# Feed-forward output tiles in pairs from seven block products of sums, in place of eight plain ones

## The reference, cut to what matters

```
x  = x + rmsnorm(mix @ w_o, g_post_mix)
hf = rmsnorm(x, g_pre_ff)
ff = square(relu(hf @ w_ff1 + b_ff1)) @ w_ff2 + b_ff2     # 1024 -> 4096 -> 1024, float32
x  = x + rmsnorm(ff, g_post_ff)
```

## Time and profile before

| | |
|---|---|
| timed runs (3) | 1230.9 us median, 1230.79 to 1233.1 |
| profiled execution | span 1229.2 us from first to last instruction; the page gives no whole time of its own for it |
| PE busy | 1222.8 us (99%), 9103 matmuls |
| DVE busy | 732.4 us (60%), 1031 instructions |
| ACT busy | 508.6 us (41%), 783 instructions |
| POOL busy | 65.2 us (5%), 129 instructions |
| chain that ended last | PE 99% |
| granted TensorE clock | 1.000 |

### The profile page before, as it was taken

The page is one execution under the profiler, slowest core; times in us unless marked ns, Lnnn a source line. Parts: engine busy times, 40 slices in busy tenths (PEclk is TensorE's granted clock), DMA queues, the critical chain, the costliest instruction groups (busy, mean ns, idle before and its releaser), DMA issues.

```text
span 1229.2 us, 23577 instructions
## 1 busy us (share of the span) xinstructions
PE 1222.8 (99%) x9103; PEld 1153.2 (94%) x9103; DVE 732.4 (60%) x1031; ACT 508.6 (41%) x783; POOL 65.2 (5%) x129
## 2 busy tenths in 40 slices
PE   9999999999999999999999999999999999999998
PEld 9999978989797897989999999999999999999998
DVE  6933788888888888887455434338543112443334
ACT  7533433353454335335443212246654223454222
POOL 4020001101100110110000000000000000000000
PEclk9999999999999999999999999999999999999999
DMA  6353225516432551623222222322322222222222
GB/s 221 103 168 138 70 81 214 195 34 239 166 118 89 215 184 34 239 104 103 93 96 87 86 86 85 144 101 62 95 100 88 85 100 70 88 91 95 86 68 73
DMA packets 40341, 141.23 MB, mean 115 GB/s; under 512 B 4788, under 2 KB 7220, under 8 KB 40168
## 3 DMA queue, kind: packets, MB, share of 16 engines
q1 hardware_dynamic: 28456, 99.02, 23.6%
q0 software_dynamic: 11424, 41.23, 9.6%
q10 hardware_dynamic: 416, 0.35, 0.1%
HBM read 118.31 MB, written 22.26 MB: 114 GB/s over the span
## 4 chain that ended last, share of the span: by engine, by line
PE 99%; issue 0%; DVE 0%; ACT 0%; POOL 0%; POOLq 0%
PE product L1655 89%; PE side L1655 10%; PE side L1840 0%; PE side L1830 0%; ACT y L1012 0%; DVE asmp L1205 0%; DVE u L1135 0%; POOL ones L446 0%; POOL eps L445 0%; DVE u L1132 0%; POOLq L2122 0%
## 5 line engine op out<-in xcount | busy, mean ns | idle before, releaser
L1029 DVE TENSOR_TENSOR wlo<-wraw,whi 128x1024 fp32r<-128x1024 f32 x176 | 214.9, 1224 | 205.8 <-ACT whi L578 191.2
L1655 PE MATMUL product<-ahi,whi 128*128 128x256 f32 (+1 forms) x1392 | 294.0, 290 | 1.3 <-DVE asmp L1205 1.3
L1655 PE MATMUL product<-ahi,wlo 128*128 128x256 f32 (+1 forms) x1392 | 290.2, 288 | 0.0
L1655 PE MATMUL product<-alo,whi 128*128 128x256 f32 (+1 forms) x1392 | 287.9, 286 | 0.0
L578 ACT ACTIVATE whi<-wraw 128x1024 fp32r<-128x1024 f32 x176 | 184.3, 1052 | 245.7 <-PE product L1655 170.5
L1655 PEld LDWEIGHTS product<-ahi,whi 128*128 128x128 f32 x1392 | 223.7, 188 | 11.6 <-issue 10.6
L1655 PEld LDWEIGHTS product<-alo,whi 128*128 128x128 f32 x1392 | 224.0, 188 | 0.0
L1655 PEld LDWEIGHTS product<-ahi,wlo 128*128 128x128 f32 x1392 | 222.8, 188 | 0.0
L1242 DVE SCALAR_TENSOR_TENSOR accp<-u,wdw,accp 128x512 f32<-128x512 f32 x240 | 163.7, 745 | 0.7 <-DVE accp L1242 0.7
L1655 PE MATMUL product<-hidhi,whi 128*128 128x288 f32 (+1 forms) x512 | 111.2, 289 | 0.0
L1655 PE MATMUL product<-hidlo,whi 128*128 128x288 f32 (+1 forms) x512 | 111.0, 288 | 0.0
(11 more groups left out here) (319 smaller groups left out, 1739.4 us busy)
## 6 DMA issues: line engine op xcount, KB each, us to landing
wraw<-in_wstream SPq DMA_DIRECT2D x176, 512.0 KB, 3.5
crg<-in_c_in POOLq DMA_DIRECT2D x32, 512.0 KB, 6.6
out_c_s<-crg POOLq DMA_DIRECT2D x32, 512.0 KB, 3.1
hb<-head_rows POOLq DMA_DIRECT2D x4, 580.0 KB, 5.3
x<-in_xT SPq DMA_DIRECT2D x4, 544.0 KB, 6.4
sgm<-in_xT SPq DMA_DIRECT2D x1, 2176.0 KB, 8.0
out_c_p<-cst POOLq DMA_DIRECT2D x4, 512.0 KB, 8.1
out_yT<-y SPq DMA_DIRECT2D x4, 288.0 KB, 2.2
```

The lines of the kernel that those rows point to most:

```text
L1029: V.tensor_tensor(wlo[:, k % RING, :, :], wraw[:, k % 2, :, :], whi[:, k % RING, :, :].bitcast(f32), ALU.subtract).then_inc(lo_done, 1)
L1655: return pe.matmul(out, lhsT, rhs, start=start, stop=stop, skip_group_check=check)
```

## The change

From the ninth feed-forward chunk on, two output tiles (two chunks, a *pair*) are made together. Weights (two tiles by two halves of the input features), activations (two halves of the features by two halves of the 544 tokens, 272 each) and outputs are seen as 2x2 blocks, and Winograd's form of Strassen's scheme is used: seven block products (`P1` to `P7`) where the plain way has eight. A block product is 4 blocks x 3 parts = 12 matmuls of 272 columns, a pair is 84 matmuls of 272 columns in place of 96 of 256 or 288. There are 28 pairs (`PAIRS`): 12 "up" (into the hidden layer) and 16 "down", in the order up, 4 down, 4 up, 4 down, 4 up, 4 down, 3 up, 4 down.

The blocks of the products are sums. POOL makes four sums of 128x512 per pair from the raw weights (`weight_sums`). ACT and DVE then split seven blocks of 128x512 per pair (`first_split`/`first_low`, `sums_`, `second_`, `last_`), where they split two chunks of 128x1024 before. For each pair of hidden tiles POOL makes four crossed blocks of 272 tokens (`cross_forms`: one instruction of 544 elements and two of 272), and ACT and DVE split seven blocks of 272 (`forms_plain`, `forms_cross`, `forms_split`, `cross_split`) in place of four. For the first layer the crossed blocks are made once: POOL scales x1 with `g_pre_ff` (8 instructions of 544 elements) and makes four sums of 1088 elements. The products are put together behind PE: for an up pair by DVE in six instructions of 272 elements and one of 816 (`u2`, `u3`, `q`, `up_last`), for a down pair by seven additions of 272 into `yacc` and a block `e`, where the first group of downs leaves most of them to ACT.

x1 (2176 KB) is stored to DRAM and read back at the end, to free its place. Raw pairs are loaded in two halves. `FRONT` is 272 in the whole kernel. The end works in halves of 272 tokens: one statistic, root and scaling each, by DVE in instructions of 1088 elements; DVE adds the residual of four tiles and POOL that of the other four; PE and ACT no longer add or copy it.

At the turn to the last group of downs (`TURN`), which needs the hidden tiles of the up pair just in front, PE does three quarters of the first four products before it waits.

```diff
-FRONT = 256
+FRONT = 272
...
+GROUPS, IN_GROUP = 4, 4
+PAIRS = []
+for _g in range(GROUPS):
+    PAIRS += [("up", _g + 1, 0)] if _g < GROUPS - 1 else []
+    PAIRS += [("down", _g, _n) for _n in range(IN_GROUP)]
+    PAIRS += [("up", _g + 1, _n) for _n in range(1, IN_GROUP)] if _g < GROUPS - 1 else []
...
+MAIN = ("P1", "P7", "P6", "P5", "P2", "P4", "P3")
+LAST = ("P1", "P7", "P6", "P2", "P4", "P5", "P3")
...
+            def pair_load(s):
+                one, two = chunks_of(s)
+                tiles = wstream[one:two + 1:two - one, :, :, :].rearrange("a p (h k) m -> h p a (k m)", h=2)
+                if s == 1:
+                    sp.wait_ge(lo_done, C_PAIRS)
+                if s >= 2:
+                    sp.wait_ge(sum_made, 4 * (s - 2) + 3)
+                    sp.wait_ge(split_lo, 5 * (s - 2) + 1)
+                sp.dma_start(raw_of(s)[:, 0, :, :].rearrange("p (a k) m -> p a (k m)", a=2), tiles[0, :, :, :]).then_inc(first_in[s % 2], 16)
+                if s >= 2:
+                    sp.wait_ge(sum_made, 4 * (s - 2) + 4)
+                    sp.wait_ge(split_lo, 5 * (s - 2) + 4)
+                sp.dma_start(raw_of(s)[:, 1, :, :].rearrange("p (a k) m -> p a (k m)", a=2), tiles[1, :, :, :]).then_inc(second_in[s % 2], 16)
...
+            pool.wait_ge(x1_ready, 2 * KT)
+            for j in range(KT):
+                pool.tensor_scalar(xg[:, j, :], yc[:, j, :], c("g_pre_ff", j).rearrange("p a -> p (a)"), None,
+                                   ALU.mult).then_inc(xg_ready, 1)
+            pool.wait_ge(xg_ready, KT)
+            near, far = xg[:, 0:KT // 2, :], xg[:, KT // 2:KT, :]
+            pool.tensor_tensor(xtf[:, 0, :, :], near[:, :, HALF:TT], near[:, :, 0:HALF], ALU.subtract).then_inc(xt_made, 1)
...
+            def cross_forms(p):
+                q = corners(cq[:, p % 2, :, :])
+                pool.wait_ge(cq_squared, p + 1)
+                if p > 0:
+                    pool.wait_ge(form_lo, 3 * p)
+                pool.tensor_tensor(tt[:, 0:4:2, :], q[:, 1:4:2, :], q[:, 0:2, :], ALU.subtract).then_inc(tt_made, 1)
+                pool.wait_ge(tt_made, 3 * p + 1)
+                pool.tensor_tensor(tt[:, 1, :], q[:, 3, :], tt[:, 0, :], ALU.subtract).then_inc(tt_made, 1)
+                pool.wait_ge(tt_made, 3 * p + 2)
+                pool.tensor_tensor(tt[:, 3, :], q[:, 2, :], tt[:, 1, :], ALU.subtract).then_inc(tt_made, 1)
...
+            def weight_sums(s):
+                raw = raw_of(s)
+                a11, a21, a12, a22 = (half_of(raw, n) for n in range(4))
+                pool.wait_ge(first_in[s % 2], 16 * (s // 2 + 2))
+                if s > 0:
+                    pool.wait_ge(split_lo, 5 * (s - 1) + 2)
+                else:
+                    pool.wait_ge(x1_moved, 16)
+                pool.tensor_tensor(s3[:, :, :], a11, a21, ALU.subtract).then_inc(sum_made, 1)
+                pool.wait_ge(second_in[s % 2], 16 * (s // 2 + 2))
+                if s > 0:
+                    pool.wait_ge(split_lo, 5 * (s - 1) + 3)
+                if s == 1:
+                    pool.wait_ge(chunk_done, C_PAIRS)
+                pool.tensor_tensor(sum_1(s)[:, :, :], a21, a22, ALU.add).then_inc(sum_made, 1)
+                pool.wait_ge(sum_made, 4 * s + 2)
+                pool.tensor_tensor(sum_2(s)[:, :, :], sum_1(s)[:, :, :], a11, ALU.subtract).then_inc(sum_made, 1)
+                pool.wait_ge(sum_made, 4 * s + 3)
+                if s > 0:
+                    pool.wait_ge(split_lo, 5 * (s - 1) + 5)
+                pool.tensor_tensor(s4[:, :, :], a12, sum_2(s)[:, :, :], ALU.subtract).then_inc(sum_made, 1)
...
+            weight_sums(0)
+            for p in range(IN_GROUP - 1):
+                cross_forms(p)
+            weight_sums(1)
+            for s in range(N_PAIRS):
+                for p in forms_due(s):
+                    cross_forms(p)
+                if s + 2 < N_PAIRS:
+                    weight_sums(s + 2)
...
+            squared(0)
             hi(0, 4, C_FF + 6)
-            for f in range(2):
-                cf = C_FF + PERHALF * f
-                sf = S_FF + S_HALF * f
...
+            squared(1)
+            forms_plain(0)
+            forms_cross(0)
+            for half in range(2):
+                act.wait_ge(xt_made, 3 + half)
+                act.activation(xthi[:, 2 * half:2 * half + 2, :, :].rearrange("p f k t -> p (f k t)"),
+                               xtf[:, 2 * half:2 * half + 2, :, :].rearrange("p f k t -> p (f k t)"), ACT.Copy).then_inc(xt_hi, 1)
+            hi(0, 4, C_FF + 7)
+            forms_plain(1)
+            forms_cross(1)
+            first_split(0)
+            squared(2)
+            sums_split(0)
+            forms_plain(2)
+            forms_cross(2)
+            second_split(0)
...
+            def up_last(s):
+                p = up_pair(s)
+                q = corners(cq[:, p % 2, :, :])
+                product_of(dve, s, "P3")
+                read(V.tensor_tensor(q[:, 1, :], u2, sums_of(s, "P3"), ALU.add), s, "P3")
+                was_read(dve, s, "P3")
+                V.tensor_tensor(q[:, 1:4, :], q[:, 1:4, :], rst_x[:, :, :], ALU.mult).then_inc(cq_ready, 1)
...
+                if up:
+                    p = up_pair(s)
+                    q = corners(cq[:, p % 2, :, :])
+                    product_of(dve, s, "P6")
+                    was_read(dve, s, "P1")
+                    read(V.tensor_tensor(u2, r1, sums_of(s, "P6"), ALU.add), s, "P6")
+                    was_read(dve, s, "P6")
+                    read(V.tensor_tensor(u3, u2, sums_of(s, "P7"), ALU.add), s, "P7")
...
+                    read(V.tensor_tensor(q[:, 3, :], u3, sums_of(s, "P5"), ALU.add), s, "P5")
+                else:
+                    was_read(dve, s, "P7")
+                    add_to(y4[:, 3, :], s, "P5")
+                if s + 1 < N_PAIRS:
+                    sums_low(s + 1)
+                for p_ in forms_due(s) if s != TURN else []:
+                    cross_split(p_)
+                if up:
+                    product_of(dve, s, "P2")
+                    read(V.tensor_tensor(q[:, 0, :], sums_of(s, "P2"), rst[:, 0:HALF], ALU.mult), s, "P2")
+                    product_of(dve, s, "P4")
+                    read(V.tensor_tensor(q[:, 2, :], u2, sums_of(s, "P4"), ALU.add), s, "P4")
+                if more:
+                    add_to(y4[:, 0, :], s, "P2")
+                    add_to(y4[:, 2, :], s, "P4")
+                if s + 1 < N_PAIRS:
+                    second_low(s + 1)
...
+            for g in range(2):
+                part = slice(HALF * g, HALF * (g + 1))
+                dve.wait_ge(tail_root, 2 * g + 2)
+                dve.wait_ge(y_gained, KT - 2 + 2 * g + 2)
+                for half in range(2):
+                    d = yacc[:, KT // 2 * half:KT // 2 * (half + 1), part]
+                    V.tensor_tensor(d, d, rst3[:, :, part].broadcast_to([P, KT // 2, HALF]), ALU.mult).then_inc(y_scaled, 1)
+                dve.wait_ge(y_scaled, 2 * g + 2)
+                d = yacc[:, KT // 2:KT, part]
+                V.tensor_tensor(d, d, x1b[:, KT // 2:KT, part], ALU.add).then_inc(out_dve, 1)
...
+                for kt in range(first, last):
+                    bhi_, blo_ = operand(s, name, kt)
+                    if kind == "down" and n == 0:
+                        pe.wait_ge(form_lo, 3 * (IN_GROUP * g + kt) + {0: 1, 1: 2, 2: 2}.get(FORM[name], 3))
+                    if s == 0 and kt == 0 and FORM[name] >= 3:
+                        pe.wait_ge(xt_lo, 2)
+                    for i, (a, b) in enumerate(((whi, bhi_), (whi, blo_), (wlo, bhi_))):
+                        ins = mm(sums_of(s, name), a[:, place // 2, KT // 2 * (place % 2) + kt, :], b,
+                                 opens and kt == 0 and i == 0, name in ("P2", "P4", "P3", "P6") and kt == KT // 2 - 1 and i == 2, True)
+                if last == IN_GROUP:
+                    ins.then_inc(product_done, 1)
...
+            for s in range(N_PAIRS):
+                if s == TURN:
+                    for name in MAIN[0:4]:
+                        seven(s, name, 0, IN_GROUP - 1)
+                for name in steps_of(s):
+                    seven(s, name, IN_GROUP - 1 if s == TURN and name in MAIN[0:4] else 0, IN_GROUP)
```

More of the change, by code:

```diff
@@ L365, in own_columns, with half_of @@
             return bass.AP(ap.tensor, ap.offset, [ap.ap[0], [NS + DEC_T, DEC_B], [1, DEC_T]])
[L367 to L382 removed]
+        def half_of(buf, place):
+            return buf[:, place // 2, KT // 2 * (place % 2):KT // 2 * (place % 2 + 1), :]
@@ new lines, in _ @@
+            weight_sums(0)
[7 more added lines that the diff above has]
+                    weight_sums(s + 2)
+            pool.wait_ge(x1_moved, 32)
+            for g in range(2):
+                part = slice(HALF * g, HALF * (g + 1))
+                pool.wait_ge(y_scaled, 2 * g + 1)
+                pool.tensor_tensor(yacc[:, 0:KT // 2, part], yacc[:, 0:KT // 2, part], x1b[:, 0:KT // 2, part],
```

(1 more changed line is left out.)

715 lines of the change are left out of this document (470 added, 245 removed).

## The result

The changed kernel takes **1292.6 us** (median of four runs, 1292.1 to 1293.3), the one before 1230.9 beside it: ratio 1.0498, interval 1.0483 to 1.0513. It is 5% slower; I had forecast 1219.4 and a range up to 1240. The sign was wrong too.

A forecast was written before the change was run, and what follows sets the result against it. PE, paced by columns, was taken to bound the kernel. Saving, up pairs, turn, start and tail gave 1229.2 - 42.0 + 17 + 4 + 6 + 3.5 = 1217.7; the run median, 1.7 above, 1219.4 us; range 1200 to 1240.

The forecast's parts named there:

- What is saved, PE's pace: All 28 pairs: 84 matmuls in place of 96, 10.50 us in place of 12.00, in sum -42.0 us.
- rival C: PE doesn't hold 0.125 us per matmul: PSUM bank waits of 0.05 us cost 10 us, some 1230; chance 0.06.
- the shared way: Up pair: SBUF reads of POOL and two-input DVE instructions exclude each other; 6.56 + 6.27 = 12.83 us, over 10.50.
- rival B: GpSimd slower than taken: k ns per element, up pair 6.56 + 3.136 k; 1243 us at k = 2.6; chance 0.23.
- The larger holds: 12.85: Up pair: of two limits, 12.83 and 11.3 us, the larger sets the time, 2.35 us over PE's.
- ring of waits: From up pair to up pair: last combination, scaling, relus, square, POOL, ACT and DVE splits in sequence, 11.3 us.
- +17: Up pairs in runs of 4, 4 and 3: 26 us over PE's time, less 9 us swallowed.
- 9 us are swallowed: Up-pair runs: DVE begins each some 3 us ahead of PE's need, so 3 x 3 us cost nothing.
- The hold: POOL's COPY of 240 elements blocks DVE for 0.24 us of its 0.39; the other 0.15 us blocks nobody.
- The start, +6: Ahead of the pairs: eighth chunk's split ready at 883, PE wants it at 876.7; 3 to 12 us by POOL's price.
- The turn, +4: Behind the last up product: crossed blocks take 9.2 us, PE has 4.9 us of matmuls; range 3.5 to 6.
- The tail, +3.5: Kernel's end: +1.2 us to the last issue, plus up to 4.4 for POOL additions excluding DVE's; 3.5 taken.

The follow-up runs named there:

- Experiments 2: Changed kernel with each pair's four weight sums written as zeros by GpSimd, without reading, instead of computed: 1261.0 us, ratio 1.0244 to the kernel before.
- 3: Changed kernel with ScalarE's `first_split` for the next pair ahead of the relus and square: 1275.7 us, ratio 1.0364 to the kernel before.
- 5: Changed kernel with weight sums written as zeros and ScalarE's `first_split` ahead of the squares: 1245.6 us, ratio 1.0117 to the kernel before.
- experiment 6: Changed kernel with weight sums and hidden tiles' crossed blocks written as zeros, and `first_split` ahead of the squares: 1230.0 us, ratio 0.9991 to the kernel before.
- experiments 9: Changed kernel with seven products for down pairs alone, up pairs plain, and another tail; token cut 272: 1240.7 us, ratio 1.0083 to the kernel before.
- 10: Seven products for down pairs alone, with tokens ahead of the feed-forward part cut into 256 and 288 columns: 1239.6 us, ratio 1.0066 to the kernel before.
- experiment 1: Changed kernel with the eight scalings of x1 moved from GpSimd to ScalarE: 1289.0 us, ratio 1.0472 to the kernel before.
- experiment 7: Changed kernel with ScalarE's six gains behind the front half's root and VectorE adding the whole residual: 1290.6 us, ratio 1.0482 to the kernel before.

## Why the prediction was wrong

- **What is saved, PE's pace** held: 10.48 us per down pair, no waiting inside them, rival C is out.
- **Which engine is the bound of an up pair** was the right question, and its terms were near: VectorE's own work 9.5 against 9.6, the shared way 12.85 against 13.65 with GpSimd's measured price (2.26 ns per element; 1.26 us for 512, 2.56 for 1088; I took 2.0). That is rival B's mechanism, at a k between mine and the 2.3 from which it decides: by the forecast's own formula k = 2.26 costs 11 x 0.8 = 9 us more and leaves a gain, so the price alone isn't what turned the sign.
- **The step that failed is "The larger holds: 12.85".** I set two limits beside each other, shared way and ring of waits, and took the larger. They are one chain: the instructions in the ring are the ones that GpSimd makes longer. And the ring lacked an edge, `first_split` behind `squared` on ScalarE, behind which VectorE can't go on; it takes in nearly all of VectorE's own work. Measured 15.54: 13.02 us of VectorE busy, waiting beside GpSimd included, and 2.52 idle in the ring, one behind the other. Experiments 2, 3 and 5 take the parts out one by one (13.54, 14.0, 11.85), and 6 brings the pair to PE's pace. The other two terms of +17 matter less: of "9 us are swallowed" some 7 were (11 x 5.04 = 55.4 us, measured 48.7 in the runs), and the first up pair, which I had as covered by its neighbours, cost 4.9.
- **The hold.** I read a hold of 0.24 of 0.39 us out of a copy. The rows of after show the whole instruction: VectorE's short instructions at 871.05, 873.60 and 876.25 end just behind GpSimd's. This is what the Trainium skill says (SBUF — State Buffer, "Who interferes with whom"), which I had put second to the row; the trace of after agrees with it. And the copy's rows had fitted a whole hold all the time. In after an instruction that has waited ends some 0.13 us sooner behind the other than its own length (L1935 1.09 for 1.22, L1977 0.87 for 1.01). The copy ended at 100.62; by that the split beside it would end at 100.62 + 1.09 = 101.71, and it ended at 101.70. I had taken a saving of the one that waits for a free part of the one that holds.
- **The start, +6.** It was 29.1. The scalings of x1 took 2.2 us each and not 0.7, and GpSimd was through with them at 867.4 where I had 857. I had the eighth chunk's split as what PE waits for, due at 876.7; it was the emptying of a PSUM slot, due at 872.95, which stood behind the same splits on VectorE. Nor had I priced what GpSimd does to VectorE's short instructions (2.6 us each for 0.3). And "the new `FRONT` moves nothing" was wrong: the fifth chunk began 1.9 us later. In experiments 9 and 10, which differ in that cut alone, it begins at 860.52 and 859.12.
- **The clock** had no term at all. Behind its long waits PE ran at 1.2 GHz for a while: 2.8 us were lost behind the start, 1.2 in the up pair shown, 2.0 at the turn (45 matmuls in 7.58 us for 5.6).
- **The turn, +4** was 9.8: PE waited 3.8 and 3.6 us there, for `hlo` L1904 and L1912. VectorE began the last combination of the last up pair at 1219.66 only, 2.1 us behind PE's last up product, since it had the splits of the next weights in front of it, and from there to the crossed blocks it took 10.6 us in place of 9.2. The lower clock is the rest.
- **The tail, +3.5** was 7.3, and 4.1 for the statistic in front of it. I had named the exclusion (+4.4 at worst) and then taken 2.3 for it; I had missed ScalarE's six gains (3.94 us) ahead of the last squares.

The forecast's sign hung on the runs of up pairs. With 15.54 in my own formula they cost 11 x 5.04 - 9 = 46 us: more than the 42 saved, before any other term.

## What to carry to other kernels

When two engines that work in order share a way, don't compare the ring of waits with the busy time and take the larger: write one period of the loop as a schedule, each engine's queue in its order, and let the lengths grow where both are busy. A stop at the start and at each change of pattern can eat a saving of 1.5 us per step; price these joints first, because experiment 6 had nearly the full saving in the loop and was no faster. And before work is taken out, look at what stands in front of what: 13.5 us were in the order alone.

## What was not expected of the hardware

- VectorE and GpSimd wait for each other's whole instruction when both have their inputs in SBUF, a VectorE COPY of 272 elements too (2.63 us, where one of 544 takes 0.43 undisturbed, in experiment 1). VectorE's additions with one input in PSUM (0.42 us for 272) are not held up.
- GpSimd's scaling by a number per partition took 1.64 us for 544 elements at its shortest and 2.17 in the mean of eight (some beside VectorE), its addition of two inputs 1.33: the instruction with one input is the slower one.
- Behind a wait of 4.5 us PE runs 2.9 us (992.19 to 995.04) at 1.2 GHz; behind the wait of 24.4 us the granted clock of the next 14.8 us is 0.81.
- Two additions of 1088 elements shared out to VectorE and GpSimd take 3.45 us; VectorE alone does both in 2.5 (experiment 7).
